# Page rings of three and two, and other offsets in the order, for the merged attention stage of a hybrid decoder layer

## What is computed

```
h = modulate(x)                                  # adaLN and RMSNorm
q, k, v, u, gv = project_in(h, w_in)             # 4 heads, two 64-wide q/k maps per head, 128-wide values
prompt:  p = softmax(mask(q k^T / 8));  o = (p[map 0] - lam * p[map 1]) v        # causal, 16 blocks of 128 queries
decode:  k_past = cache_k[page_table]; v_past = cache_v[page_table]
         p = softmax([q k_past^T, mask(q k_new^T)] / 8);  o = (p[map 0] - lam * p[map 1]) [v_past, v_new]
x = x + gate * (concat(norm(o), chunked spatial gating MLP of u, gv) @ w_out)
x = x + gate * hierarchical MoE(modulate(x)) ;  final RMSNorm
```

## Time and profile before

| | |
|---|---|
| runs | median 3481.39 us of 3 (3467.72 to 3481.64) |
| the profiled execution | 3463.04 us, its span 3461.5 us |
| PE, DVE, ACT, POOL busy over the span | 2957.7, 1378.3, 971.3, 443.0 us |
| mean granted clock of TensorE | 0.936 |
| first and last transpose of key pages | 824.6 and 1865.7 us from the span's start |
| key page, value page, from issue to landing (median) | 4.1 us, 4.5 us |

### The profile page before, as it was taken

One profiled execution on the slowest core, in us unless ns is written; L12 is line 12 of the kernel. 1 busy time (PEld: TensorE's weight loads), 2 busy tenths in 40 slices (PEclk: granted clock), 3 DMA queues, 4 the chain that ended last, 5 costly groups with the idle time before them and its releaser, 6 DMA issues. The chain is left out here.

```text
span 3461.5 us, 54799 instructions
## 1 busy us (share of the span) xinstructions
PE 2957.7 (85%) x17860; PEld 1499.6 (43%) x17860; DVE 1378.3 (40%) x2706; ACT 971.3 (28%) x2216; POOL 443.0 (13%) x781
## 2 busy tenths in 40 slices
PE   5799999996798899999997899729999999889960
PEld 1244444444565566666655355423333333333320
DVE  2223322223666777877886445460000000000009
ACT  0122222223455566666654011100111111001114
POOL 0000000001332222222221000000000000000015
PEclk8899999997999999999999999859999999999985
DMA  9410110005998787786664653215452848999838
GB/s 346 155 37 36 45 45 36 36 30 198 323 334 285 273 281 253 254 268 216 230 211 147 192 172 133 78 57 185 156 179 97 303 155 303 400 375 343 307 141 336
DMA packets 278852, 688.24 MB, mean 199 GB/s; under 512 B 29056, under 2 KB 30336, under 8 KB 278520
## 3 DMA queue, kind: packets, MB, share of 16 engines
q1 hardware_dynamic: 208592, 456.18, 38.3%
q0 software_dynamic: 64528, 218.54, 17.6%
q10 hardware_dynamic: 5528, 11.02, 0.9%
HBM read 605.26 MB, written 80.37 MB: 198 GB/s over the span
## 5 line engine op out<-in xcount | busy, mean ns | idle before, releaser
L420 PE MATMUL z<-w_in_sb,hT 128*128 128x512 f32 (+1 forms) x1360 | 601.0, 602 | 0.7 <-ACT hT L455 0.7
L420 PEld LDWEIGHTS z<-w_in_sb,hT 128*128 128x128 f32 (+1 forms) x1360 | 254.8, 189 | 322.8 <-issue 320.4
L833 POOL DMA_DIRECT2D v_ring<-cache_v x512 | 276.2, 539 | 789.9 <-issue 788.1
L910 PE MATMUL ps_turned<-ident,k_ring 128*128 128x128 f32 x2048 | 300.4, 285 | 57.5 <-DMA k_ring<-cache_k 48.2
L1855 PE MATMUL e_gu<-wu,xT 128*64 128x512 f32 x1344 | 303.3, 605 | 20.4 <-DMA wu<-w_exp_up 20.4
L1855 PE MATMUL e_gu<-wg,xT 128*64 128x512 f32 x1344 | 301.4, 601 | 21.0 <-DMA wg<-w_exp_gate 20.3
L1883 PE MATMUL e_y<-wd,ehT 128*64 128x512 f32 x1344 | 299.4, 598 | 12.8 <-DMA wd<-w_exp_down 11.3
L910 PEld LDWEIGHTS ps_turned<-ident,k_ring 128*128 128x128 f32 x2048 | 229.6, 144 | 169.4 <-issue 87.8
L1008 ACT ACTIVATE kTs<-ps_turned 128x512 f32<-128x512 f32 x384 | 227.7, 599 | 205.3 <-PE ps_turned L910 204.7
L1926 DVE TENSOR_TENSOR hh<-e_gu,sg 128x512 f32<-128x512 f32 x42 | 29.0, 691 | 622.6 <-PE e_gu L1855 622.6
L1034 ACT ACTIVATE p_probs<-p_scores,neg_chunk_max 128x512 f32<-128x512 f32 (+3 forms) x320 | 196.5, 622 | 81.9 <-DVE neg_chunk_max L1151 81.2
(11 more groups left out here) (302 smaller groups left out, 3347.0 us busy)
## 6 DMA issues: line engine op xcount, KB each, us to landing
v_ring<-cache_v POOLq DMA_DIRECT2D x512, 256.0 KB, 4.5
k_ring<-cache_k SPq DMA_DIRECT2D x512, 256.0 KB, 4.1
wg<-w_exp_gate SPq DMA_DIRECT2D x33, 2048.0 KB, 10.5
wu<-w_exp_up SPq DMA_DIRECT2D x33, 2048.0 KB, 11.8
wd<-w_exp_down SPq DMA_DIRECT2D x33, 2048.0 KB, 9.9
scratch_y<-y SPq DMA_DIRECT2D x42, 512.0 KB, 9.8
kT<-w_ada SPq DMA_DIRECT2D x6, 2048.0 KB, 16.1
V<-w_ada SPq DMA_DIRECT2D x6, 2048.0 KB, 16.2
```

What stands on the lines that cost most here:

```text
L420: last = pe.matmul(z[0:R, c, :], hT[:, k, 0:R], w[:, k, c * 512:(c + 1) * 512], start=(k == 0), stop=(k == KD - 1))
L833: eng.dma_start(ring[:, u, j, :], cache[0, ds(page, 1)].rearrange(layout)).then_inc(arrived[u], 16)
L910: last = pe.transpose(turned("turn_k", n, h)[:, j * P:(j + 1) * P], k_ring[:, n % K_RING, j, h * P:(h + 1) * P], ident[:])
```

## The change

The key ring gets three slots and the value ring two (before: two and three). The memory for both together is the same. SP's first loads are the key pages of steps 0, 1 and 2 and the queries of blocks 0 and 1. `load_k` in the order is for step n + 1 + K_RING, so it runs one step further ahead.

The offsets of `STEP_AT` and `HEAD_AT` are all replaced. Before, the even and the odd steps of a pair had the same offsets; now each has its own. So the order of the operations on PE, DVE, ACT and SP is another one, with the same operations, shapes and counts.

```diff
-K_RING, V_RING = 2, 3
+K_RING, V_RING = 3, 2
...
 STEP_AT = (
-    (((0.69, 0.89, 1.28, 2.04), 0.7, 2.08, 0.15, 2.49, 0.98, 3.98, 4.74, 1.8),
-     ((0.69, 0.89, 1.28, 2.04), 0.7, 2.08, 0.15, 2.49, 0.98, 3.98, 4.74, 1.8)),
-    (((0.04, 0.21, 0.69, 3.6), 0.79, 2.33, 0.02, 2.37, 1.92, 2.73, 4.65, 2.61),
-     ((0.04, 0.21, 0.69, 3.6), 0.79, 2.33, 0.02, 2.37, 1.92, 2.73, 4.65, 2.61)),
-    (((0.06, 0.13, 2.32, 3.31), 0.74, 2.49, 0.64, 1.16, 0.5, 2.89, 4.9, 3.55),
-     ((0.06, 0.13, 2.32, 3.31), 0.74, 2.49, 0.64, 1.16, 0.5, 2.89, 4.9, 3.55)),
-    (((0.06, 1.0, 1.45, 4.31), 0.73, 1.93, 1.23, 3.81, 0.95, 1.68, 4.9, 3.44),
-     ((0.06, 1.0, 1.45, 4.31), 0.73, 1.93, 1.23, 3.81, 0.95, 1.68, 4.9, 3.44)),
+    (((0.17, 0.19, 0.42, 0.95), 0.12, 2.25, 0.1, 0.82, 0.76, 1.35, 4.9, 0.02),
+     ((0.71, 1.35, 2.32, 2.42), 0.73, 0.02, 0.02, 1.52, 2.55, 2.9, 4.37, 1.18)),
+    (((0, 0.0, 0.61, 2.53), 0.1, 1.41, 0.02, 3.05, 0.93, 2.1, 4.9, 2.88),
+     ((-0.38, -0.02, 0, 0), 0.31, 1.91, 0.14, 0.65, 2.21, 3.96, 4.9, 1.74)),
+    (((0.08, 0.16, 0.96, 4.0), 0.05, 1.98, 0.17, 0.28, 0.46, 0.74, 4.84, 4.17),
+     ((0, 0.06, 1.44, 3.77), 0.51, 0.66, 0.82, 1.79, 0.06, 2.38, 4.9, 0.77)),
+    (((0.24, 0.27, 3.34, 4.65), 0.02, 2.0, 0.53, 3.62, 0.91, 1.7, 4.84, 3.53),
+     ((0.74, 1.58, 3.2, 4.15), 0.59, 1.9, 0.82, 2.09, 3.03, 4.68, 4.9, 2.13)),
 )
 HEAD_AT = (
-    (2.04, 1.0, 1.26, 4.28, 1.1, 2.79, 0.13, 6.41, 3.57, 0.02, 2.31, 1.94),
-    (0.37, 1.0, 1.4, 1.33, 2.28, 0.02, 2.95, 3.66, 5.16, 0.02, 4.77, 0.02),
-    (1.39, 1.0, 0.51, 1.03, 1.96, 2.44, 2.09, 2.38, 2.76, 0.06, 3.01, 3.03),
-    (0.38, 1.0, 0.35, 1.13, 2.46, 2.49, 1.57, 1.99, 2.09, 0.31, 0.97, 1.98),
+    (0.02, 1.26, 4.33, 3.28, 1.47, 10.73, 0.07, 24.28, 3.45, 0.29, 10.01, 1.11),
+    (0.39, 0.98, 0.99, 1.58, 1.61, 3.86, 4.94, 1.26, 2.13, 0.39, 10.75, 0.78),
+    (0.72, 1.2, 0.45, 0.39, 0.02, 7.87, 2.34, 1.58, 4.93, 0.48, 1.92, 0.22),
+    (0.66, 1.01, 0.25, 1.16, 0.26, 10.77, 2.3, 1.76, 1.26, 0.39, 2.04, 1.23),
 )
...
-                load_k(0)
-                load_q(0)
-                load_k(1)
-                load_q(1)
+                for n in range(K_RING):
+                    load_k(n)
+                    if n < 2:
+                        load_q(n)
```

## The result

The changed kernel takes 3435.1 us (median of 4 runs, 3433.5 to 3439.2) against 3481.5 (4 runs, 3467.7 to 3482.3): a ratio of 0.988, with a 95% interval of 0.9859 to 0.990. That is 46.4 us faster by the medians and some 42 by the ratio, which is formed from the means; 3443 was forecast. The profiled execution of the changed kernel took 3439.2 us with a span of 3437.6, 23.9 us less than the span before.

The account below looks back on a forecast made before the run. PE was taken to bound the attention stage, standing still 94.7 us over its four quarters. The terms 23 + 10 + 5 + 0 = 38 us, off the median 3481.4, gave 3443 us; range 3404 to 3475.

Parts of the forecast that it names:

- The floor and its two kinds of waits: Attention stage: PE's busy time is a floor; its 94.7 us idle, mostly page waits and sequence-end waits, bound the gain.
- Three key slots, second quarter: Second quarter: the third key slot covers the key waits, winning 23 of 24.9 us, at least 10.
- Three key slots, first quarter: First quarter: key waits shrink only as far as DMA allows, 10 us won, bounds 22 and nothing.
- the DMA limit: First quarter: DMA engines are full at 353 GB/s, so 65.5 MB take 186 us and 22 us is the most.
- the value path: First quarter: 5.75 us to the fourth page's issue plus landing, 10.85 to 12.85 us against pairs near 12.4; rarely waits.
- Rival C: Waits change sides: value pages late where keys were; nothing from first quarter, 10 us from second, 3471 us; chance 0.19.
- The loads and the rest: First quarter: queries wanted two nominal units earlier with `load_q` unmoved, within 5 us; nothing changes outside the stage.
- Two value slots afterwards: After the first quarter the smaller value ring costs nothing; by a skill rule, an estimated 3.58 us longer at sequence ends.
- The order between sequence ends: Third and fourth quarters: new order wins 5 of 11.5 us idle; bounds all of them and a loss of 16.
- Rival D: Slower: the chain from `p_score` through two `p_exps` takes over in the third and fourth quarters, 3512 us; chance 0.09.
- One sign of failure: The prediction fails if PE waits for `p_exps` by more than 0.5 us a pair.
- The order at sequence ends: Long waits at sequence ends, 31.2 us in all, stay; gain nothing, bounds all of it and a loss of 10.

Follow-up runs that it names:

- short_sum_three_three_q: Changed kernel with `sum` cut to one step of sixteen, three key and three value slots, `load_q` at 30 units in place of 16: 3370.4 us, 0.9691.
- rings_q: Kernel before with three key and two value slots, old offsets, and `load_q` at 30 units in place of 16: 3431.6 us, 0.9869.
- q_early: Changed kernel with `load_q` put 30 nominal units before its head in place of 16: 3427.3 us, 0.9842 of the kernel before.
- two_two: Kernel before, old offsets, with the value ring cut from three slots to two: 3475.5 us, 0.9985.
- short_sum: Changed kernel with the two long DVE operations of `sum` cut to one step of sixteen: 3386.8 us, 0.9723 of the kernel before.

## Why the prediction held, and where it did not

**The floor and its two kinds of waits.** Right in what it named: idle time of PE fell by 28.7 us in the changed kernel, and busy time rose by 1.0. Too low as a bound: 94.7 us was called about all there is to win, but PE's busy time holds time at the lower clock, and short_sum_three_three_q runs the four quarters 104 us shorter (937.3 against 1041.4) with the same matmuls, though with less work on DVE.

**Three key slots, second quarter.** Forecast 23 us, measured 22.7 of idle time (the other 4.5 of the 27.1 are busy time, some of it work that now falls into the third quarter); 23.3 with the ring alone once queries don't wait (rings_q). The mechanism and the size were right. That the new order cuts the same waits was not foreseen; it changes little beside the ring.

**Three key slots, first quarter.** Forecast 10, measured nothing. Two steps failed. One is the DMA limit, "there the DMA engines are full": 373 GB/s were reached with a third value slot. That the limit was none stood in the profile before already, in the bandwidth by slices of its page (40 slices of 86.5 us; the 35th and 36th lie in the expert stage):

```profile
GB/s 346 155 37 36 45 45 36 36 30 198 323 334 285 273 281 253 254 268 216 230 211 147 192 172 133 78 57 185 156 179 97 303 155 303 400 375 343 307 141 336
```

The other step is the value path, of which it was said that it "rarely waits". Its form was right: in the wait shown above, the fourth page is issued 6.1 us after the products two steps earlier began, where 5.75 was counted, and its landing takes 7.4, where the longest was 7.1. But 11.9 us of value waits took the key waits' place, 3.7 of them after POOL's pause, which no one had counted. Rival C came true in this quarter and in no other. What the Trainium skill, *DMA: Bandwidth & Descriptors*, Specifications, gives as a limit for one core, about 358 GB/s as half of a stack's 716, is passed by the 373 of that run and by the 400 of the slice above, with this kernel on one core; the measurement decides. So the sentence that the trace agrees holds for the earlier trace rows and not for the whole profile.

**The loads and the rest.** The heads of the first quarter want their queries two units earlier while `load_q` stays; that was put "within 5 us". The waits for queries were 6.3 us, against 3.7 before, and with the clock behind them q_early shows 11.8. So the term for the first quarter was spent here and on the value ring.

**Two value slots afterwards.** Right: 0.8 us of value waits in the second quarter of the changed kernel, none listed later, and 1 inside the interval of two_two. The lengthening by 3.58 us at sequence ends did not show either: during the two long operations of `sum` in the first quarter (936.6 to 942.6) value pages landed in 5.4 to 6.0 us, beside a median of 5.2.

**The order between sequence ends.** Forecast 5 in the two late quarters; measured 1.0 by their lengths and 3.0 by PE's idle time, all in the fourth. Some of the 3.0 is the ring's: 1.5 us of key waits there are gone. Rival D's chain is visible but small, in the fourth quarter 5.0 us for 4.2 before. One sign of failure came by the letter: in the third quarter PE waits 12.6 us for `p_exps`, 0.8 us a pair where 0.5 was the bound. In short_sum 3.2 us of that stay, so the rest belongs to the sequence ends.

**The order at sequence ends.** Right: 31.2 us before, and after it 3.6, 9.1, 9.4 (the 12.6 without those 3.2) and 7.6, which is 29.7, with 4.31 us where the count gave 4. What the count left out is the clock, which by short_sum adds 0.6 us to each microsecond of such waits.

**The sum.** 38 us were forecast, and the stage gave 27.7 to its last key transpose, all of the shortfall in the first quarter and the order. The medians differ by 46.4 all the same, because the profiled execution of before was 18.5 us under its median and that of the changed kernel 4.1 over its own. No row here shows where the other executions of the kernel before spend that time: it may be in the stage or outside it, and this stays open. So that 3443 came within 8 us of 3435 is in part luck: the term for the first quarter was too high, and a difference between executions went the other way.

## What to carry to other kernels

When a ring gets a slot, look for what is late next on the same engine, and price it with the work behind it: here value pages and queries ate the gain of one quarter that a table of waits had promised. A block of seven microseconds on one engine every sixteen steps cost more than the new order saved, and cutting it into pieces was worth more than half as much as the whole change. A bandwidth read from one stretch is no limit while another stretch of the same profile passes it, or until a run with more buffers fails to. And when an order changes, compare idle times and counts of work beside the lengths of windows, because work can move over their borders.

## What the runs showed of the hardware

A wait of PE of 4.31 us was followed by 6.6 us at a mean granted clock of 0.64, between TensorE's levels of 1.2 and 2.4 GHz, though PE was busy all through. Over the stage, without the two long operations of `sum`, 33.5 us of idle time went and 19.9 us of busy time with them.

Pages of 256 KB from two queues reached 373 GB/s with three slots on either side, at a DMA share of 1.02 as the windows give it; with two and three slots a stretch at 0.98 moved 353. Share and bytes rose together, so a share of 0.98 did not mean that the engines were full.

POOL, issuing value pages every 1.15 us, stood still at the same page in each of the fourteen profiles, for 3.8 to 6.1 us from one issue to the next, and again after every 108 or 112 pages. With two value slots the longest wait for values of the changed kernel followed the first of them (3.65 us); with three, no run lists a wait for values in that quarter.
